# A hybrid decoder step on eight cores: post-norm sums and gamma at the eviction, other paces for the background work, spatial gating inside the u stage, other first and last tiles

## The reference

```python
h = rmsnorm(x, g_pre_mix)
a, u, v, ga, gb = split(h @ w_in, [512, 1024, 1024, 1024, 1024])
ya = per_group_linear(trailing_mean_w(a) - a, w_pg) * pool_scale
v = layernorm(gelu(v), ln_g, ln_b)
yb = gelu(u) * (tril(W_s[head]) @ v + b_s[head])       # per chunk of 128 tokens
m = sigmoid(ga) * (ya @ w_branch_a) + sigmoid(gb) * (yb @ w_branch_b)
x = x + rmsnorm(m @ w_out, g_post_mix)
f = square(relu(rmsnorm(x, g_pre_ffn) @ w_up)) @ w_down
x = x + rmsnorm(f, g_post_ffn)
```

## Time and profile before

| | |
|---|---|
| median of 3 runs | 3928.03 us (3906.65 to 3934.39) |
| the profiled execution | 3905.28 us, its span on the slowest core (core 6) 3903.9 us |
| spans of the eight cores | 3884.3 to 3903.9 us |
| TensorE busy | 3690.1 us, 95% |
| VectorE, ScalarE, GpSimd busy | 1657.9 us (42%), 1415.0 us (36%), 314.0 us (8%) |
| the 16 DMA engines, mean | 67.6% for GpSimd's queue, 15.6% for SP's |

### The profile page before, as it was taken

How to read it: one execution, slowest core, us unless ns; L and a number is a source line. 1 busy time by engine, 2 the same in 40 slices (tenths; PEclk the granted TensorE clock), 3 DMA queues, 4 the chain that set the end, 5 groups by cost and what they waited for, 6 DMA issues and landing times.

```text
span 3903.9 us, 63096 instructions; the slowest of 8 cores (3884.3 to 3903.9 us)
## 1 busy us (share of the span) xinstructions
PE 3690.1 (95%) x22132; PEld 2113.6 (54%) x22273; DVE 1657.9 (42%) x3585; ACT 1415.0 (36%) x2730; POOL 314.0 (8%) x364
## 2 busy tenths in 40 slices
PE   5999899998999989999899999999989999999997
PEld 3555554555455565455455556545555555655563
DVE  4655740414366574041335756404225474631231
ACT  3444441523334444142233443423324344342231
POOL 0000000000000000000000000000000000000000
PEclk9999999998999999999999999999999999999998
...
GB/s 173 133 121 143 165 174 137 163 110 180 114 150 117 155 171 176 124 170 115 179 132 140 127 140 182 178 105 171 139 156 132 135 132 158 173 164 103 172 145 136
DMA packets 429109, 575.23 MB, mean 147 GB/s; under 512 B 12564, under 2 KB 375620, under 8 KB 428736
## 3 DMA queue, kind: packets, MB, share of 16 engines
q0 software_dynamic: 368256, 377.51, 67.6%
q1 hardware_dynamic: 60544, 193.67, 15.6%
...
## 4 chain that ended last, share of the span: by engine, by line
PE 85%; DVE 6%; DMA 5%; issue 3%; ACT 1%; DVEq 0%; SPq 0%; ACTq 0%; POOLq 0%
PE ps L329 83%; DMA wslot<-w_up 2%; PE ps L396 2%; DMA xin<-yp 1%; DMA wslot<-w_down 1%; DMA xin<-w_pg 1%; DVE oT L430 1%; DVE ps L876 1%; DVE R L921 1%; PE ps L869 1%; DVE htok L383 0%; DVE oT L425 0%; DVE htok L387 0%; DVE ps L936 0%; DVE R L888 0%
## 5 line engine op out<-in xcount | busy, mean ns | idle before, releaser
L329 PE MATMUL ps<-hT,wslot 128*128 128x384 bf16 (+1 forms) x11520 | 1869.4, 320 | 53.8 <-ACT R L774 31.3
L329 PEld LDWEIGHTS ps<-hT,wslot 128*128 128x128 bf16 x11520 | 1121.6, 99 | 690.1 <-issue 78.8
L329 PE MATMUL ps<-wslot,R 128*128 128x512 bf16 x5324 | 1170.0, 379 | 19.3 <-DVE ps L936 5.0
L329 PEld LDWEIGHTS ps<-wslot,R 128*128 128x128 bf16 x5440 | 531.7, 98 | 654.3 <-issue 18.6
L990 DVE TENSOR_TENSOR R<-R 128x384 bf16<-128x384 bf16 (+1 forms) x768 | 259.4, 345 | 1176.8 <-ACT R L988 1173.7
L988 ACT ACTIVATE R<-ps 128x384 bf16<-128x384 f32 (+1 forms) x768 | 359.4, 472 | 451.6 <-PE ps L329 449.8
L329 PE MATMUL ps<-R,wslot 128*128 128x384 bf16 (+1 forms) x2304 | 413.4, 317 | 14.7 <-DVE R L888 14.7
L1031 ACT ACTIVATE oT<-ps 128x512 f32<-128x512 f32 x136 | 81.2, 597 | 858.2 <-PE ps L329 858.0
L907 ACT ACTIVATE sg<-ps 128x384 bf16<-128x384 f32 (+1 forms) x384 | 180.1, 473 | 466.5 <-PE ps L329 296.4
L329 PEld LDWEIGHTS ps<-R,wslot 128*128 128x128 bf16 x2304 | 223.4, 98 | 141.9 <-issue 17.7
L341 ACT ACTIVATE sqj<-oT 128x1024 bf16<-128x1024 f32 x267 | 280.5, 1051 | 33.2 <-DVE oT L430 33.2
(11 more groups left out here) (101 smaller groups left out, 1744.5 us busy)
## 6 DMA issues: line engine op xcount, KB each, us to landing
...
yp<-oT SPq DMA_DIRECT2D x128, 512.0 KB
...
```

The costliest lines, as they stand in the source:

```text
L329: last = e.matmul(ps[b][:, 0:N], lhsT=lhs_fn(k), rhs=rhs_fn(k), start=(start and k == 0), stop=(stop and k == kc - 1))
```

## The change

- **Eviction.** `evict_out` replaces both copies (L966, L1031) for the out- and the down-projection. ScalarE squares the 512 columns straight out of PSUM and sums them into one of two columns per tile, and VectorE multiplies the same 512 columns by the gamma row into oT. `sum_halves` adds the two sums. `post` then does oT * rr + x in one instruction. The gamma row of post-norm is loaded when a phase starts.
- **Background.** A list for 6 tiles has 18 steps instead of 26 in the mix kind; in both kinds the posts come at steps 4 to 14 (11 to 21 before), loads of x start at once and have a sixth slot. Ticks carry weights: 1.3 per a group, 0.15 per v and u group, 1.4 and 1.6 per branch of the gates. In ffn phases the background spreads over the up-projection and three slabs of the first down half, and the drain stands ahead of the fourth.
- **Spatial.** A spatial group follows each u group from the seventh on (10 of 16), the last 6 stand in gate a. The sample row's normalisation for the spatial product (`samp_v`) follows u group 5; its output (`samp_out`, `samp_out2`) moves to gate a. Pooling work is spread thinner in prompt v groups.
- **Start and end.** x tile 0 and the gamma row are asked for first; slab 0 waits until tile 0 has landed, the other three until tile 5 has. The six scales are worked out ahead, three tiles are transposed, then comes the first half of the a stage, then the other three tiles. VectorE copies those transposes. In the last phase `finish_scale` stands between the two halves of the eviction, and x loads begin at the first down half's fourth slab.

```diff
+        def evict_out(b, i, half, between=None):
+            q = nxt("sqj", 2)
+            S.op("act", [("ps", b)], [("sqj", q), ("ssh", half, i)],
+                 lambda e: e.activation(out=sqj[q][:, 0:512], in_=ps[b][:, 0:512], func=AF.Square,
+                                        accum_out=ssh[half][:, i:i + 1]))
+            if between is not None:
+                between()
+            S.op("dve", [("ps", b), ("grow", 0)], [("oT", i, half), ("ps", b)],
+                 lambda e: e.tensor_tensor(out=oT[:, i, half * 512:(half + 1) * 512], in0=ps[b][:, 0:512],
+                                           in1=grow[0][:, half * 512:(half + 1) * 512], op=ALU.mult))
+
+        def sum_halves(n):
+            S.op("dve", [("ssh", h, i) for h in range(2) for i in range(n)], [("ssq", i) for i in range(n)],
+                 lambda e: e.tensor_tensor(out=ssq[:, 0:n], in0=ssh[0][:, 0:n], in1=ssh[1][:, 0:n], op=ALU.add))
...
-        def post1(i):
-            S.op("dve", [("oT", i, 0), ("oT", i, 1), "rr", ("grow", 0)], [("oT", i, 0), ("oT", i, 1)],
+        def post(i, tile, slot):
+            S.op("dve", [("oT", i, 0), ("oT", i, 1), "rr", slot[2]], [("oT", i, 0), ("oT", i, 1)],
                  lambda e: e.scalar_tensor_tensor(out=oT[:, i, :], in0=oT[:, i, :], scalar=rr[:, i:i + 1],
-                                                  in1=grow[0][:], op0=ALU.mult, op1=ALU.mult))
-
-        def post2(i, tile, slot):
-            S.op("dve", [("oT", i, 0), ("oT", i, 1), slot[2]], [("oT", i, 0), ("oT", i, 1)],
-                 lambda e: e.tensor_tensor(out=oT[:, i, :], in0=oT[:, i, :], in1=slot[1][:], op=ALU.add))
+                                                  in1=slot[1][:], op0=ALU.mult, op1=ALU.add))
...
+            def start():
+                sum_halves(n)
+                rsqrt(n, kind == 1)
+            ld(0)
+            ld(1)
+            if more:
+                P.add(0, lambda: load_rows(1, 2 if kind == 0 else 0, l if kind == 0 else l + 1))
             if kind == 1:
                 P.add(0, lambda: eps_term(tiles))
+            P.add(1, start)
+            p = 4
             for i in range(n):
-                P.add(i, lambda i=i: square_acc(i, ssq[:, i:i + 1], ("ssq", i)))
-            P.add(n + 1, lambda: rsqrt(n, kind == 1))
-            p = n + 2
-            for i in range(n):
-                P.add(p - 3 + 2 * i, lambda i=i: ld(i))
-                P.add(p + 2 * i, lambda i=i: post1(i))
-                P.add(p + 3 + 2 * i, lambda i=i: post2(i, tiles[i], slots[i]))
-                P.add(p + 6 + 2 * i, lambda i=i: stat(i))
-            if kind == 0:
-                h_steps(P, p + 5, tiles, False, 2)
-            else:
-                e = p + 6 + 2 * (n - 1)
+                if i >= 2:
+                    P.add(p - 6 + 2 * i, lambda i=i: ld(i))
+                P.add(p + 2 * i, lambda i=i: post(i, tiles[i], slots[i]))
+                if more:
+                    P.add(p + 3 + 2 * i, lambda i=i: stat(i))
+            if more and kind == 0:
+                h_steps(P, p + 1, tiles, False, 2)
+            elif more:
+                e = p + 3 + 2 * (n - 1)
                 P.add(e + 2, lambda: rsqrt(n, False))
-                h_steps(P, e + 3, tiles, True, 1)
...
-            set_pace(80)
+            W_A, W_V, W_U, W_GA, W_GB = 1.3, 0.15, 0.15, 1.4, 1.6
+            set_pace(8 * W_A + 2 * NT * W_V + 16 * W_U + 16 * W_GA + 15 * W_GB)
+            load_rows(0, 1, l)
...
+            def samp_v():
+                i = NT - 1
+                S.op("act", [vs[2], "vrs", "vnm"], b3row(i),
+                     lambda e: e.activation(out=B3[:, i, :], in_=vs[1][:, :], func=AF.Identity,
+                                            scale=vrs[:, i:i + 1], bias=vnm[:, i:i + 1]))
+
+            def samp_out():
+                i = NT - 1
+                S.op("act", [vs[2], "vrs", "vnm"], [vs[2]],
+                     lambda e: e.activation(out=vs[1][:, :], in_=vs[1][:, :], func=AF.Identity,
...
                 a_stage(slab, n, n0, N)
+                if n == 0 and between is not None:
+                    between()
...
+            SLAG = 6
+            for idx in range(16):
+                h, n = idx // 2, idx % 2
+                if idx % 8 == 0:
+                    slab = take()
+                u_group(slab, h, n, *subs[n])
+                tick(W_U)
+                if idx % 8 == 7:
+                    release(slab)
+                if samp and idx == SLAG - 1:
+                    samp_v()
+                if idx in (9, 11):
+                    wpg_stage((idx - 9) // 2, *subs[(idx - 9) // 2])
+                if idx >= SLAG:
+                    spatial((idx - SLAG) // 2, (idx - SLAG) % 2, *subs[(idx - SLAG) % 2])
...
-            for idx in range(19):
+            rows = None
+            for idx in range(18):
                 if idx < 16:
                     gate(idx, "a")
-                if idx >= 2 and idx - 2 < 16:
+                if idx < SLAG:
+                    q = 16 - SLAG + idx
+                    spatial(q // 2, q % 2, *subs[q % 2])
+                if idx >= 2:
                     branch_a(idx - 2)
-                    tick()
-                if idx >= 3:
-                    spatial(jn[idx - 3][0], jn[idx - 3][1], *subs[jn[idx - 3][1]])
+                    tick(W_GA)
+                if samp and idx == 9:
+                    rows = samp_out()
+                if samp and idx == 14:
+                    samp_out2(rows)
...
-                    tick()
+                    tick(W_GB)
...
-                    S.op("act", [("ps", b)], [("oT", i, half)],
-                         lambda e: e.activation(out=oT[:, i, half * 512:(half + 1) * 512], in_=ps[b][:, 0:512], func=AF.Copy))
+                    evict_out(b, i, half)
...
-            set_pace(58)
+            load_rows(0, 3, l)
+            set_pace(64 + 3 * NT * 1.35 - 3)
...
-                        tick()
+                        tick(1.0)
                 release(slab)
-            drain_bg()
...
+                    if half == 0 and ks == 3:
+                        drain_bg()
+                        if final:
+                            eps_term(tiles)
+                            for i in range(NT):
+                                xs_slots[i] = xload(tiles[i], False)
...
-                            b = banks[i]
-                            S.op("act", [("ps", b)], [("oT", i, half)],
-                                 lambda e: e.activation(out=oT[:, i, half * 512:(half + 1) * 512], in_=ps[b][:, 0:512],
-                                                        func=AF.Copy))
-                            if final:
-                                half_stat(i, half)
-                                if half == 1:
-                                    finish_scale(i)
-                                    if i > 0:
-                                        post1(i - 1)
-                                        post2(i - 1, tiles[i - 1], xs_slots[i - 1])
+                            if final and half == 1:
+                                evict_out(banks[i], i, half, lambda: finish_scale(i))
+                                if i > 0:
+                                    post(i - 1, tiles[i - 1], xs_slots[i - 1])
+                            else:
+                                evict_out(banks[i], i, half)
...
+        S.dma([], [("oT", 0, 0), ("oT", 0, 1)], oT[:, 0, :], x_src(0))
         S.dma([], ["ident"], ident[:], c_ident)
-        for i in range(2):
+        load_rows(1, 0, 0)
...
-            S.dma([], [("oT", i, 0), ("oT", i, 1)], oT[:, i, :], x_src(i))
+        pump(1, (S.lw[("oT", 0, 0)],))
+        pump(NSLOT, (S.lw[("oT", 5, 0)],))
...
+        def first_h(i):
+            q = nxt("htok", 2)
+            okeys = [("oT", i, 0), ("oT", i, 1)]
+            S.op("dve", okeys + [("fs", i), ("grow", 1)], [("htok", q)],
+                 lambda e: e.scalar_tensor_tensor(out=htok[q][:, :], in0=oT[:, i, :], scalar=rr[:, i:i + 1],
+                                                  in1=grow[1][:], op0=ALU.mult, op1=ALU.mult))
+            trans_h(i, q, "dve")
...
+            first_scale(i)
+        for i in range(3):
+            first_h(i)
+
+        def second_part():
+            for i in range(3, 6):
+                first_h(i)
```

152 lines of the change are left out of this document (51 added, 101 removed).

## The result

| | before | changed |
|---|---|---|
| median of 20 runs | 3912.51 us | 3946.92 us |
| fastest | 3905.81 us | 3932.87 us |
| slowest core of the profiled execution | 3903.9 us | 3936.7 us |
| spans of the other cores | from 3884.3 us | from 3896.9 us |
| granted clock, mean, by core | 0.986 to 0.988 | 0.976 to 0.980 |

The ratio is 1.0084, with a 95% interval of 1.0060 to 1.0109; it compares runs that no die at a lower clock disturbed, while the medians of the table are over all 20 runs. The forecast was 3800 us, ratio 0.97.

What follows compares the result with a forecast made beforehand. No engine's load binds; TensorE's 214 us of standing and the lower clock after pauses can be won. Gains and losses sum to 107.5 us off 3905.3, giving 3798, plus 2: 3800 us; own range 3765 to 3835, with rivals 3762 to 3850.

Steps and rivals of the forecast that it cites:

- priced at 0 since its reader comes a whole stage later: Gamma row loaded at each phase's start, ahead of the block's x loads on SP's queue: cost 0.
- 2 instead of 3 operations ... 0: Pooling per v group of prompt blocks, taken as GpSimd work with GpSimd at 8% of the span: cost 0.
- part 3: Ten of 16 spatial groups moved into the u stage: gain 9 in sample blocks, losses 7 and 10 elsewhere.
- 40 -> 31: Four sample u stages: excess falls from 40 to 31 us, gain 9, with a new wait of about 5.7 us.
- loss 7: Prompt u stages: the first spatial group waits 1.1 us for normalised v rows in 7 blocks, 7 us lost.
- saved 10: Kernel start: six tiles at 3.9 us each instead of 5.55 save 10 us, bounds 2 and 14.
- loss 10: Layer 0, block 0: preparation forced after the v normalisation makes PE wait 12 us against 2 today, 10 us lost.
- 62 -> 9: Sample up-projections of layers 0 to 2: excess falls from 62 to 9 us, gain 53, as h waits nearly go.
- Rival (a): Sample ffn: DMA takes the wait's place and half the up excess stays; +25, 3825 us, chance 18%.
- priced neutral: Eviction: VectorE multiply of 0.7 us, 1.4 per tile against 1.28 saved; VectorE neutral, direct gain small.
- Rival (d): Eviction into oT waits for that tile's store to land, 8.7 us in 24 phases; about 4007 us, chance 5%.
- (c): Loads stay as late on SP's in-order queue; only spatial, start and tail count, -20: 3885 us, chance 7%.

Runs made afterwards that it cites:

- Experiment 1: Changed kernel with the sample blocks' post-norm gamma row asked for after the two state_pool loads; ratio 0.9979 to the kernel before.
- experiment 2: Changed kernel with three pooling operations per v group in prompt blocks instead of two; ratio 1.0042 to the kernel before.
- experiment 7: Kernel of experiment 5 with all 16 spatial groups in gate a, samp_v moving too; 3794.0 us, ratio 0.9711 to the kernel before.
- 9: Changed kernel with only all 16 spatial groups put in gate a, samp_v moving too; ratio 0.9922 to the kernel before.
- experiment 4: Changed kernel with pool_scale's load given its own semaphore key, so not waiting for ln_g; ratio 1.0054 to the kernel before.
- experiment 5: Changed kernel with the repairs of Experiment 1, experiment 2 and experiment 4, plus v weight 1.0 in the very first block; ratio 0.9893 to the kernel before.
- experiment 10: Kernel of experiment 7 with the old even paces in the very first block, replacing its v weight; ratio 0.9703 to the kernel before.
- 8: Kernel of experiment 5 with all feed-forward background steps within the up stage, drained at its end; ratio 0.9848 to the kernel before.
- 12: Kernel of experiment 7 with the old even mix paces in all blocks; ratio 0.9712 to the kernel before.
- 11: Kernel of experiment 7 with the old eviction: ScalarE copy, whole-row squares in the background, two-pass post; ratio 0.9888 to the kernel before.

## Why the prediction was wrong

- **The gamma row, "priced at 0 since its reader comes a whole stage later".** This is the step that failed first: 52 us. The sentence asked who reads the row, and weighed a wait of the eviction. It did not ask what the load itself waits for (the last reader of the old row, at the end of the phase before) nor what stands behind it on SP's queue (the state_pool loads, wanted at the end of the a stage). Experiment 1 gives back all of it in these stages.
- **Pooling, "2 instead of 3 operations ... 0".** It was priced by GpSimd's busy share, although the pooling instructions run on VectorE, ahead of the v normalisation that part 3 had just put on TensorE's path: 16 us in three stages by experiment 2.
- **Spatial in the u stage, "40 -> 31" and "loss 7".** The waits were sized rightly: 5.3 to 5.4 us (forecast 5.7) in sample blocks and 1.1 to 1.2 (forecast 1.1) in prompt blocks. Wrong was the balance. The forecast compared with the 7.72 us wait of the earlier trace rows, which stood behind the sample row's passes on ScalarE; with those and spatial both out of the way the sample u stage takes its plain 18.6 us (7 and 9), so the four stages held 40 us to be won and spatial's own wait took their place. Against that choice the placement costs 50 to 55 us (experiments 7 and 9), of which a part is time in gate b and at the lower clock.
- **The start, "saved 10" against "loss 10".** First transposes and first matmuls did come sooner, the first a stage at 26 instead of 43, and the forced preparation cost its 12.9 us. The forecast named late slabs but did not follow the small loads: pool_scale behind ln_g and w_pg behind the slabs, some 11 us by experiment 4. With weight 1.0 for the v groups besides (5) the first v stage took 23.7 us, against 36.3 and 37.9 by experiments 2 and 4 alone, so the forced preparation could be avoided. The first block's gates are longer by 11 us; even paces there give back 8 of 13 us in experiment 10, and the rest is open.
- **Up stages, "62 -> 9".** Some 27 us were saved, not 53. The 62 came from the slowest core, whose three stages took 285.7 us; on the middle core they took 274.6, 51 over the plain price, and 24 of these are left where 9 were forecast. Rival (a) was right in mechanism: slabs of w_up are late (22.6 us in the changed kernel, 32.9 on core 3 of experiment 7) at a DMA share of 1.01 to 1.06, and the chain holds one w_up load of 34 to 40 us in each of the three stages. The second block's up gained 16, not 8, but down, priced at nothing, gave back 10. "The residual add begins sooner" fits all runs, spreading gains nothing (8).
- **Weighted paces in the gates.** The forecast credited them with 32 us together with the shorter list. In the second prompt blocks they have no part (12): gate a's 10 us come with the new eviction (11), gate b's 10 us with neither, which leaves the earlier and shorter list. In sample blocks they are worth 10 us.
- **The eviction, "priced neutral".** Its multiply took 0.691 us (forecast 0.7) and TensorE never waited for a bank of the eviction, but without it the sum is up to 59 us longer (11): 33 in gate a, 14 behind the sample out-projections, 10 in sample v. It was under-rated, so the good part of the change was bigger than forecast.
- **The tail** gave 8 us (forecast 7.5), the cycle 2.39 us (2.4).
- **The signs named ahead.** Those of the new waits came (L864, 12.86 us in layer 0, 12.0 us for htok, a tail of 11.2 us). The sample up-projections stood at 82 to 84 us and not near 77, and v of the first block began at 61.6 and not near 45.

With the four repairs of experiment 5 and spatial in gate a the kernel takes 3794.0 us. That it lies near the forecast of 3800 is luck: it is another kernel than the one forecast, and some terms were too large and the eviction too small.

Rival (d), stores that hold up the eviction, is absent from the waits. (c) came nearest in kind (loads late because SP's queue is in order) but had other loads and no loss against the kernel before.
